# Eight weight matrices laid out slab by slab in HBM instead of row by row: a two-block kernel with 192 streamed 1 MB weight loads and 512 gathers

## The chip, the cores and the metric

The kernel runs on one core of a Trainium2 chip. The time is the device time of the whole program in microseconds (us), and less is better. One execution was also profiled, and the rows below are read from its trace.

## What is computed

One sequence of 256 tokens of width 2048, in fp32, goes through two blocks, one after the other.

```python
# first block
h = rms_norm(x, norm_gain);  proj = h @ w_in                      # 2048 x 8192
y_conv = rms_norm(short_gated_conv(...)) * silu(z_conv)           # 3 taps, width 1024
y_attn = rms_norm(moba_attention(q, k, v)) * silu(z_attn)         # 8 heads of 128
x = x + concat(y_conv, y_attn) @ w_out                            # 2048 x 2048
# second block
h = rmsnorm(x, norm_mix);  proj = h @ w_in_2                      # 2048 x 7168
merged = gate0 * (conformer_conv(...) @ conv_w_out)               # 1024 x 2048
       + gate1 * ((z @ ssm_w_val) * sigmoid(z @ ssm_w_gate))      # z from a grouped SSM
x = x + merged @ w_out_2                                          # 2048 x 2048
h = rmsnorm(x, norm_ffn)
q = h @ peer_w_q                                                  # 2048 x 2048
# per token 8 heads x top 16 experts of 16384: rows of u and v tables, 8 KB each
act = gelu(h . u_tab[expert]);  x = x + sum(gates * act * v_tab[expert])
return rmsnorm(x, norm_final)
```

## The kernel before

The 256 tokens are two tiles of 128. Everything but the last product keeps the channels on the partitions and the 256 tokens in the free dimension. The five engines run programs of their own that meet at semaphores; the order of all work is written out by hand.

**Weights.** The eight matrices `w_in`, `w_out`, `w_in_2`, `conv_w_out_2`, `ssm_w_val_2`, `ssm_w_gate_2`, `w_out_2` and `peer_w_q_2` are streamed through four buffers of 1 MB, `w_raw` (in the profile `weight_raw`, 128 partitions x 2048 floats), in 192 loads. A load is a slab: all rows of 128 columns of a matrix of 2048 rows, or of 256 columns of one of 1024 rows. `load` (L353) on SP's queue waits until TensorE has finished with the slab four before (`proj_done`), and issues one DMA. In HBM the matrices lie row by row, so that a partition gets 16 pieces of 512 bytes (8 of 1 KB for the matrices of 1024 rows). ACT (L766) makes a rounded copy `w_high` of most slabs, DVE (L1084) the rest `w_low`, in place, and TensorE multiplies three times (L495, L496, L499); 58 of the 216 tiles, those of `peer_w_q` among them, are plain fp32 products (L475).

**Start.** SP issues the two 1 MB loads of `x`, the first four slabs of `w_in` without a wait, then 16 loads of 32 KB and two of 256 KB for the SSM matrices, and the fifth slab once TensorE has finished the first. ACT's queue meanwhile issues 14 short loads of norm gains, biases and convolution taps (13 at L770 with 1 to 32 rows of 512 bytes, and at L789 the taps with 124 partitions of two rows), and three for the SSM. TensorE transposes `x` (L538), then waits for all 14 (`vec_in`, 16 * 14) and transposes them (L544); behind it in its program stand the 16 sums of squares of the first norm (L516), on which all else depends.

**The turn to the experts.** While TensorE makes the 16 tiles of `peer_w_q`, the keys of a head are scored as soon as its tiles are there (L716), ACT copies the scores (L766), and DVE picks the 16 best pairs (`head_picks`, from L1530). After heads 0, 3 and 7 the picks go out as row numbers (`experts`, L1570). POOL gathers one u row for each of 128 tokens with one indirect DMA of 1 MB (L435), and DVE makes its dot product (L1588). DVE's order is head 0, dots 0 to 2, head 1, dots 3 to 6, head 2, dots 7 to 9, head 3, dots 10 to 12, and so on. The gathers go to 7 row buffers at first and to 11 once the four weight buffers are free. As the slabs of `peer_w_q` are on the way meanwhile, POOL holds a gather back until a certain slab has landed:

```python
UNPACED = 3
def slab_before(s):
    return min(6 + (s - UNPACED) // 2, 15)
...
if UNPACED <= s < EARLY_PICKS:
    slab = SLAB_WQ + slab_before(s)
    pool.wait_ge(raw_landed[slab % NSLAB], 16 * (slab // NSLAB + 1))
```

Gathers 3 and 4 wait for slab 6 of `peer_w_q`, 5 and 6 for slab 7, 7 and 8 for slab 8, to 15. All in all there are 512 gathers: 128 of u and 128 of v for each tile of tokens. Half the v rows are summed by TensorE (L752) and half by DVE (L1606).

Of the kernel before, what the change touches and what calls it, by code (L numbers as in the profile page):

```python
# [13 lines left out]
P = 128  # L14
# [4 lines left out]
HALF = D // 2  # L19
KH = HALF // P  # L20
# [49 lines left out]
SLAB = 2048  # L70
NSLAB = 4
# [5 lines left out]
TILE_IN = 0  # L77
TILE_OUT = TILE_IN + 64
TILE_IN2 = TILE_OUT + 16
TILE_GATE = TILE_IN2 + 24  # L80
TILE_CV = TILE_IN2 + 56
TILE_VG = TILE_CV + 16
TILE_OUT2 = TILE_VG + 32
TILE_WQ = TILE_OUT2 + 16
# [41 lines left out]
def val(u):  # L126
# [3 lines left out]

BRANCH = [("glu", 0), ("sig", 0), ("glu", 1), ("sig", 1), *(("ssm", n) for n in range(4)),
          *((kind, n) for n in range(2, 8) for kind in ("glu", "sig")), *(("ssm", n) for n in range(4, 8))]
BRANCH_COL = {"glu": 0, "sig": HALF, "ssm": 2 * HALF}
BRANCH_SLOT = {"glu": GLU0, "sig": SIG0, "ssm": SSM0}
SUBK0, SUBT0 = 40, 16
TOPK0 = 48
# [43 lines left out]
def build(nc, d):  # L180
    ctx = ExitStack()
    with ctx:
        def sb(name, shape, dt=F32):
            return ctx.enter_context(nc.sbuf_tensor(name, shape, dt))

        def sem(name):
            return ctx.enter_context(nc.semaphore(name))
# [7 lines left out]
        w_raw = sb("weight_raw", [P, NSLAB, SLAB])  # L195
# [81 lines left out]
        raw_landed = [sem(f"raw_landed{b}") for b in range(NSLAB)]  # L277
# [59 lines left out]
        @block.sync  # L337
        def _(sp):
            for t in range(TT):
                sp.dma_start(x_tok0[:, t, :], d["x"][0, t * P:(t + 1) * P, :]).then_inc(x_in[t], 16)  # L340
            def matrix(name):
                return d[name][0].rearrange("(k p) n -> p k n", p=P)

            w_in, w_out, w_in2, w_val, w_gate, w_cv, w_out2, w_q = (matrix(n) for n in (
                "w_in", "w_out", "w_in_2", "ssm_w_val_2", "ssm_w_gate_2", "conv_w_out_2", "w_out_2", "peer_w_q_2"))

            def load(w, col, last_tile):

                at = len(slab_ends)
                if at >= NSLAB:  # L350
                    sp.wait_ge(proj_done, slab_ends[at - NSLAB])
                n = SLAB // w.shape[1]
                sp.dma_start(w_raw[:, at % NSLAB, :].rearrange("p (k n) -> p k n", n=n),  # L353
                             w[:, :, col:col + n]).then_inc(raw_landed[at % NSLAB], 16)
                slab_ends.append(last_tile)

            slab_ends = []
            for t in range(32):
                if t == NSLAB:
                    sp.wait_ge(cdiag_cleared, 1)  # L360
                    for c, name in enumerate(("ssm_c_re_2", "ssm_c_im_2")):
                        src = d[name][0].rearrange("(a g) h p -> g h a p", g=8)
                        for g in range(8):
                            sp.dma_start(c_diag[GCH * g:GCH * g + GCH, c, :, STATE * (g % 2):STATE * (g % 2) + STATE],
                                          src[g]).then_inc(c_in, 16)

                    sp.wait_ge(misc_done, M_X + 8)
                    for c, name in enumerate(("ssm_b_re_2", "ssm_b_im_2")):
                        sp.dma_start(b_nat[:, c, :, :], d[name][0].rearrange("(r s) p h -> (s p) r h", s=2)).then_inc(b_in, 16)
                load(w_in, 4 * HALF + P * t, TILE_IN + t + 1)  # L370
            for part in (0, 2, 1, 3):
                for t in range(KH):
                    load(w_in, part * HALF + P * t, TILE_IN + len(slab_ends) + 1)
            for t in range(16):
                load(w_out, P * t, TILE_OUT + t + 1)

            for t, (kind, n) in enumerate(BRANCH):
                load(w_in2, BRANCH_COL[kind] + P * n, TILE_IN2 + t + 1)
            for t in range(32):
                load(w_in2, 3 * HALF + P * t, TILE_GATE + t + 1)  # L380

            for j in range(8):
                load(w_cv, 256 * j, TILE_CV + 2 * j + 2)
            for u in range(8):
                for m, w in enumerate((w_val, w_gate)):
                    load(w, 256 * u, TILE_VG + 4 * u + 2 * m + 2)
            for t in range(4):
                load(w_out2, P * t, TILE_OUT2 + t + 1)

            sp.wait_ge(merged, KD)  # L390
            sp.dma_start(subk, d["peer_sub_keys_2"][0].rearrange("h c n e -> n (h c) e")).then_inc(subk_in, 16)
            for t in range(4, 16):
                load(w_out2, P * t, TILE_OUT2 + t + 1)
            for t in range(16):
                load(w_q, P * t, TILE_WQ + t + 1)

            sp.wait_ge(picks_ready, len(HEAD_PARTS) + 1)
            sp.dma_start(gain_b, d["norm_final_2"].partition_broadcast(P)).then_inc(gain_in, 16)
            for t in range(TT):
                for half in range(2):  # L400
                    cols = slice(half * HALF, (half + 1) * HALF)
                    sp.wait_ge(normed, 2 * t + half + 1)
                    sp.dma_start(d["out"][0, t * P:(t + 1) * P, cols], y_tok[:, t, cols]).then_inc(stored, 16)
            sp.wait_ge(stored, 16 * 2 * TT)
# [1271 lines left out]
]  # L1676


# [15 lines left out]
```

## Time and profile before

| | us |
|---|---|
| median of three runs | 2563.43 (2560.07 to 2563.51) |
| the profiled execution | 2563.8 |
| its span in the trace | 2562.0 |
| TensorE busy in the span | 1758.3 |
| VectorE (DVE) busy | 1840.4 |
| ScalarE (ACT) busy | 560.9 |
| GpSimd (POOL) busy | 871.9 |

The span runs from the first to the last instruction of the trace; 1.8 us of the execution lie around it. All times of rows are counted from the start of the span. A busy share over the whole span says little here, since the kernel has two halves of different kinds: up to about 1315 us the products, after that the gathers.

### The profile page before, as it was taken

What the parts mean: (1) busy time and instruction counts of PE and PEld (TensorE: products, weight loads), DVE (VectorE), ACT (ScalarE), POOL (GpSimd) and SP (SyncE); (2) the same over time, 40 slices, a digit from 0 to 9 for tenths busy, and PEclk for the clock granted to TensorE, in tenths of its full rate; (3) what the DMA queues carried; (4) which work ended last, traced back from release to release, by engine and by line L of the source; (5) the groups of instructions that cost most, each with busy time, mean ns of one, the idle gap of its engine ahead of it and who ended that gap; (6) DMA issues with size and microseconds to landing.
All of it is one profiled execution on the core that took longest, in us unless ns stands there. A gap on an engine that the chain in (4) does not pass through costs nothing. (4 is left out here: it accounts for less than half of the span.)

```text
span 2562.0 us, 25369 instructions
## 1 busy us (share of the span) xinstructions
PE 1758.3 (69%) x10238; PEld 1400.0 (55%) x10238; DVE 1840.4 (72%) x2417; ACT 560.9 (22%) x813; POOL 871.9 (34%) x525
## 2 busy tenths in 40 slices
PE   8999999999999979999950001776760000177776
PEld 7999999998899969999840000222220000022222
DVE  6655677476799896654799998778459999844444
ACT  4345555421036413433110000000000000000000
POOL 0000000000000000000348887565658888755552
PEclk9999999999999989999985555999995555599999
DMA  7655655655566535665999999999999999999997
GB/s 201 181 165 165 165 165 144 170 151 145 148 169 172 162 107 153 184 190 137 363 370 390 422 422 421 421 421 422 422 421 423 421 422 422 422 422 422 422 421 305
DMA packets 458296, 747.44 MB, mean 292 GB/s; under 512 B 22130, under 2 KB 391236, under 8 KB 392260
## 3 DMA queue, kind: packets, MB, share of 16 engines
q0 software_dynamic: 73728, 536.90, 50.5%
q1 hardware_dynamic: 383776, 208.68, 29.3%
q8 instruction: 81, 1.33, 0.2%
q10 hardware_dynamic: 676, 0.24, 0.0%
q14 instruction: 35, 0.29, 0.0%
HBM read 743.68 MB, written 2.10 MB: 291 GB/s over the span
## 5 line engine op out<-in xcount | busy, mean ns | idle before, releaser
L495 PE MATMUL ps<-operand_high,weight_high 128*128 128x256 f32 x2272 | 564.9, 288 | 6.7 <-DVE operand_low L1341 3.1
L496 PE MATMUL ps<-operand_low,weight_high 128*128 128x256 f32 x2272 | 555.3, 284 | 0.0
L1084 DVE TENSOR_TENSOR weight_low<-weight_raw,weight_high 128x2048 fp32r<-128x2048 f32 x142 | 325.3, 2291 | 199.2 <-ACT weight_high L766 198.7
L495 PEld LDWEIGHTS ps<-operand_high,weight_high 128*128 128x128 f32 x2272 | 438.3, 193 | 12.1 <-issue 7.0
L496 PEld LDWEIGHTS ps<-operand_low,weight_high 128*128 128x128 f32 x2272 | 438.6, 193 | 2.6 <-issue 2.2
L752 PE MATMUL ps<-weight_raw,residual_t 128*128 128x512 f32 x368 | 170.7, 607 | 327.2 <-ACT residual_t L1043 269.0
L427 POOL IOTA slots<- 128x16 f32 x1 | 0.1, 144 | 1071.9 <-DVE slots L1482 1071.9
L752 PE MATMUL ps<-rows_high,residual_t 128*128 128x512 f32 x192 | 91.4, 620 | 347.5 <-ACT residual_t L1043 316.0
L766 ACT ACTIVATE weight_high<-weight_raw 128x2048 fp32r<-128x2048 f32 x142 | 270.7, 1906 | 166.1 <-PE ps L499 101.7
L752 PEld LDWEIGHTS ps<-weight_raw,residual_t 128*128 128x128 f32 x368 | 67.0, 192 | 430.9 <-ACT residual_t L1043 339.1
L499 PE MATMUL ps<-operand_high,weight_low 128*128 128x256 f32 x2272 | 298.6, 283 | 1.7 <-DVE weight_low L1084 1.6
L499 PEld LDWEIGHTS ps<-operand_high,weight_low 128*128 128x128 f32 x2272 | 283.9, 192 | 2.2 <-DVE weight_low L1084 2.1
L752 PEld LDWEIGHTS ps<-rows_high,residual_t 128*128 128x128 f32 x192 | 35.8, 196 | 402.6 <-ACT residual_t L1043 344.1
L475 PE MATMUL ps<-slots,weight_raw 128*128 128x256 f32 x1088 | 240.1, 383 | 18.6 <-DVE slots L1457 17.1
L475 PEld LDWEIGHTS ps<-slots,weight_raw 128*128 128x128 f32 x1088 | 208.0, 192 | 49.7 <-issue 20.4
L1588 DVE SCALAR_TENSOR_TENSOR weight_raw<-weight_raw,work 128x2048 f32<-128x2048 f32 x85 | 193.3, 2290 | 13.8 <-DMA weight_raw<-in_peer_u,slots 13.5
L435 POOL DMA_INDIRECT weight_raw<-in_peer_u,slots x85 | 172.0, 2023 | 33.6 <-issue 24.4
L1588 DVE SCALAR_TENSOR_TENSOR slots<-slots,work 128x2048 f32<-128x2048 f32 x75 | 170.5, 2289 | 14.9 <-DMA slots<-in_peer_u,slots 14.7
L1606 DVE SCALAR_TENSOR_TENSOR work<-weight_raw,slots,work 128x2048 f32<-128x2048 f32 x45 | 105.8, 2352 | 91.9 <-DMA weight_raw<-in_peer_v,slots 91.6
L435 POOL DMA_INDIRECT slots<-in_peer_u,slots x75 | 145.7, 1943 | 61.9 <-DMA weight_raw<-in_peer_w_q 26.8
L819 ACT ACTIVATE slots<-ps 128x256 f32<-128x256 f32 x136 | 52.1, 383 | 500.7 <-PE ps L499 250.3
L435 POOL DMA_INDIRECT weight_raw<-in_peer_v,slots x91 | 129.1, 1419 | 93.6 <-PE ps L752 67.3
(220 smaller groups left out, 2510.5 us busy)
## 6 DMA issues: line engine op xcount, KB each, us to landing
weight_raw<-in_w_in SPq DMA_DIRECT2D x120, 1024.0 KB, 6.2
weight_raw<-in_w_out SPq DMA_DIRECT2D x32, 1024.0 KB, 5.9
weight_raw<-in_peer_w_q SPq DMA_DIRECT2D x16, 1024.0 KB, 12.0
weight_raw<-in_conv_w_out SPq DMA_DIRECT2D x8, 1024.0 KB, 5.6
weight_raw<-in_ssm_w_val SPq DMA_DIRECT2D x8, 1024.0 KB, 5.6
weight_raw<-in_ssm_w_gate SPq DMA_DIRECT2D x8, 1024.0 KB, 5.6
work<-in_x SPq DMA_DIRECT2D x2, 1024.0 KB, 6.2
out_y<-work SPq DMA_DIRECT2D x4, 512.0 KB, 5.2
```

What stands on the lines that cost most here:

```text
L427: nc.gpsimd.iota(iota16, pattern=[[1, 16]], base=0, channel_multiplier=0, allow_small_or_imprecise_dtypes=True).then_inc(zero_ready, 1)
L435: nc.gpsimd.indirect_dma_start(rows[b], None, table, bass.IndirectOffsetOnAxis(ap=picks[:, col:col + 1], axis=0),).then_inc(gathered[b], 16)
L475: mm = nc.tensor.matmul(ps_p[:, t % PSLOTS, :], w[:, k, :], operand[:, k, :], start=(k == order[0]), stop=(k == order[-1]))
L495: nc.tensor.matmul(out, high[:, k, :], o_high[:, place(k), :], start=(k == order[0]), stop=False)
L496: nc.tensor.matmul(out, high[:, k, :], o_low[:, place(k), :], start=False, stop=False)
L499: mm = nc.tensor.matmul(out, low[:, k, :], o_high[:, place(k), :], start=False, stop=(k == order[-1]))
L752: mm = nc.tensor.matmul(ps_v[:, c, :], diag[:, i // 2 % 16, :], rows[b][:, c * 512:(c + 1) * 512], start=False, stop=False, skip_group_che ...
L766: return nc.scalar.activation(dst, src, ACT.Copy)
L819: return nc.scalar.activation(dst, ps_p[:, n % PSLOTS, :], func, **kw).then_inc(proj_freed, 1)
L1084: v.tensor_tensor(w_low[:, s % NSLAB, :], w_raw[:, s % NSLAB, :], w_high[:, i % NHIGH, :], ALU.subtract).then_inc(w_low_ready, 1)
L1588: v.scalar_tensor_tensor(out=rows[b], in0=rows[b], scalar=1.0, in1=h_tok[:, t, :], op0=ALU.mult, op1=ALU.mult, accum_out=dots[:, at:at + 1 ...
L1606: v.scalar_tensor_tensor(out=y_tok[:, t, :], in0=rows[b], scalar=pick_w[:, at:at + 1], in1=y_tok[:, t, :], op0=ALU.mult, op1=ALU.add).then ...
```

## The change

The host lays each of the eight matrices out anew, once, ahead of the launch: slab after slab, and within a slab partition after partition with its 2048 floats (8 KB) in a row. The kernel's load takes slab number `slab` as it lies. The same bytes arrive at the same places of the same buffers; the order of the loads, their number and size, and all waits are the same, and no other load is changed.

```diff
-            def matrix(name):
-                return d[name][0].rearrange("(k p) n -> p k n", p=P)
-
-            w_in, w_out, w_in2, w_val, w_gate, w_cv, w_out2, w_q = (matrix(n) for n in (
+            w_in, w_out, w_in2, w_val, w_gate, w_cv, w_out2, w_q = (d[n] for n in (
                 "w_in", "w_out", "w_in_2", "ssm_w_val_2", "ssm_w_gate_2", "conv_w_out_2", "w_out_2", "peer_w_q_2"))
 
-            def load(w, col, last_tile):
+            def load(w, slab, last_tile):
 
                 at = len(slab_ends)
                 if at >= NSLAB:
                     sp.wait_ge(proj_done, slab_ends[at - NSLAB])
-                n = SLAB // w.shape[1]
-                sp.dma_start(w_raw[:, at % NSLAB, :].rearrange("p (k n) -> p k n", n=n),
-                             w[:, :, col:col + n]).then_inc(raw_landed[at % NSLAB], 16)
+                sp.dma_start(w_raw[:, at % NSLAB, :], w[slab]).then_inc(raw_landed[at % NSLAB], 16)
                 slab_ends.append(last_tile)
...
-                load(w_in, 4 * HALF + P * t, TILE_IN + t + 1)
+                load(w_in, 4 * KH + t, TILE_IN + t + 1)
...
+def in_slabs(w):
+
+    kts = w.shape[0] // P
+    n = SLAB // kts
+    return w.reshape(kts, P, w.shape[1] // n, n).transpose(2, 1, 0, 3).reshape(-1, P, SLAB)
...
-        a = np.ascontiguousarray(inputs[name])
+        a = np.ascontiguousarray(in_slabs(np.asarray(inputs[name])[0]) if name in _IN_SLABS else inputs[name])
```

The other calls of `load` go from columns to slab numbers in the same way.

## Rows read from the trace of the kernel before

**Rows 1.** The page's DMA queues: packets, MB, share of 16 engines' span

```profile
q0 software_dynamic: 73728, 536.90, 50.5%
q1 hardware_dynamic: 383776, 208.68, 29.3%
```

**Rows 2.** Windows: stretch, busy us (instructions) by engine, clock, DMA share, GB/s

```profile
200.00:300.00 100.00, 100.00 (x812) 98.20 (x811) 63.20 (x60) 56.33 (x79) 0.00 (x0) 1.00 0.61 167
...
2000.00:2200.00 200.00, 0.00 (x0) 0.00 (x0) 183.06 (x160) 0.00 (x0) 172.55 (x80) 0.50 1.01 422
```

**Rows 3.** Waits of TensorE up to 1300 us: total us, times, longest

```profile
PE ps L475 <- DVE slots L1457: 17.1, 1, 17.1
PE ps L538 <- DMA work<-in_x: 7.6, 2, 5.9
```

**Rows 4.** DMA issues of the whole span: count, KB each, median us to landing

```profile
weight_raw<-in_w_in SPq DMA_DIRECT2D x120, 1024.0 KB, 6.2
...
residual_t<-in_norm_final SPq DMA_DIRECT2D x1, 1024.0 KB, 9.1
```

**Rows 5.** Line 353 from 1160 to 1290: who waited for it (us, times), and landing

```profile
  POOL slots L435: 26.8, 3
...
  PEld ps L475: 0.3, 1
...
DMA to landing us min/median/max: 5.7/12.0/22.6
```

**Rows 6.** Line 353 from 1220 to 1228: slab 7 of `peer_w_q`

```profile
L353 SPq DMA_DIRECT2D weight_raw<-in_peer_w_q x1: 368/368/368, 1222.2 to 1222.2; - x1
...
DMA to landing us min/median/max: 16.8/16.8/16.8
```

**Rows 7.** Queues in the window 1230 to 1232 (q0 the gathers, q1 SP's)

```profile
q0 software_dynamic: 108, 0.77, 91.6%
q1 hardware_dynamic: 108, 0.06, 9.1%
```

**Rows 8.** POOL's timeline: gathers 5 and 35 (start, us, line, idle before)

```profile
1239.22 1.52 POOL L435 DMA_INDIRECT slots<-in_peer_u,slots  x1 [15.39 <-DMA weight_raw<-in_peer_w_q]
...
1344.90 2.74 POOL L435 DMA_INDIRECT operand<-in_peer_u,slots  x1 [11.26 <-DVE operand L1588]
```

**Rows 9.** DVE's timeline: dot 0, dot 5, and the first instruction of head 3

```profile
1223.65 2.29 DVE L1588 SCALAR_TENSOR_TENSOR rows_high<-rows_high,work 128x2048 f32<-128x2048 f32 x1 [6.17 <-DMA rows_high<-in_peer_u,slots]
...
1248.56 2.29 DVE L1588 SCALAR_TENSOR_TENSOR slots<-slots,work 128x2048 f32<-128x2048 f32 x1 [6.41 <-DMA slots<-in_peer_u,slots]
...
1265.83 0.29 DVE L1530 MAX8 slots<-residual_t 128x8 f32<-128x128 f32 x1
```

**Rows 10.** ACT's timeline: the copy of head 3's scores

```profile
1261.15 0.60 ACT L766 ACTIVATE residual_t<-ps 128x512 f32<-128x512 f32 x1 [0.51 <-PE ps L716]
```

**Rows 11.** ACT's queue in windows 2 to 6, 7.3 to 11, 11 to 13

```profile
q10 hardware_dynamic: 64, 0.02, 1.8%
...
q10 hardware_dynamic: 190, 0.06, 6.5%
...
q10 hardware_dynamic: 287, 0.12, 29.2%
```

**Rows 12.** SP's queue in the window 3 to 7.6, which holds `x` alone

```profile
q1 hardware_dynamic: 250, 1.90, 98.9%
```

**Rows 13.** PE's timeline at the start: parameter transposes, sums of squares

```profile
16.11 0.83 PE L544 MATMUL ps<-ident,slots 90*128 90x90 f32 x4 [0.87 <-DVE residual_t L1070]
16.78 7.08 PE L516 MATMUL ps<-scan_ws,ones 128*128 128x256 f32 x32
```

**Rows 14.** Line 789, the load of the taps: who waited for it

```profile
  PEld ps L544: 1.1, 1
```

**Rows 15.** Windows after an idle stretch of TensorE (columns as in rows 2)

```profile
938.00:940.00 2.00, 2.00 (x6) 1.58 (x5) 1.97 (x5) 0.00 (x0) 0.00 (x0) 0.50 0.00 0
...
944.00:946.00 2.00, 2.00 (x11) 1.77 (x10) 2.00 (x4) 0.00 (x0) 0.00 (x0) 1.00 0.00 0
```

More of the change, by code:

```diff
@@ L132 @@
           *((kind, n) for n in range(2, 8) for kind in ("glu", "sig")), *(("ssm", n) for n in range(4, 8))]
-BRANCH_COL = {"glu": 0, "sig": HALF, "ssm": 2 * HALF}
+BRANCH_SLAB = {"glu": 0, "sig": KH, "ssm": 2 * KH}
 BRANCH_SLOT = {"glu": GLU0, "sig": SIG0, "ssm": SSM0}
@@ L369, in _ @@
                         sp.dma_start(b_nat[:, c, :, :], d[name][0].rearrange("(r s) p h -> (s p) r h", s=2)).then_inc(b_in, 16)
-                load(w_in, 4 * HALF + P * t, TILE_IN + t + 1)
+                load(w_in, 4 * KH + t, TILE_IN + t + 1)
             for part in (0, 2, 1, 3):
                 for t in range(KH):
-                    load(w_in, part * HALF + P * t, TILE_IN + len(slab_ends) + 1)
+                    load(w_in, part * KH + t, TILE_IN + len(slab_ends) + 1)
             for t in range(16):
-                load(w_out, P * t, TILE_OUT + t + 1)
+                load(w_out, t, TILE_OUT + t + 1)
             for t, (kind, n) in enumerate(BRANCH):
-                load(w_in2, BRANCH_COL[kind] + P * n, TILE_IN2 + t + 1)
+                load(w_in2, BRANCH_SLAB[kind] + n, TILE_IN2 + t + 1)
             for t in range(32):
-                load(w_in2, 3 * HALF + P * t, TILE_GATE + t + 1)
+                load(w_in2, 3 * KH + t, TILE_GATE + t + 1)
             for j in range(8):
-                load(w_cv, 256 * j, TILE_CV + 2 * j + 2)
+                load(w_cv, j, TILE_CV + 2 * j + 2)
             for u in range(8):
                 for m, w in enumerate((w_val, w_gate)):
-                    load(w, 256 * u, TILE_VG + 4 * u + 2 * m + 2)
+                    load(w, u, TILE_VG + 4 * u + 2 * m + 2)
             for t in range(4):
-                load(w_out2, P * t, TILE_OUT2 + t + 1)
+                load(w_out2, t, TILE_OUT2 + t + 1)
             sp.wait_ge(merged, KD)
@@ L392, in _ @@
             for t in range(4, 16):
-                load(w_out2, P * t, TILE_OUT2 + t + 1)
+                load(w_out2, t, TILE_OUT2 + t + 1)
             for t in range(16):
-                load(w_q, P * t, TILE_WQ + t + 1)
+                load(w_q, t, TILE_WQ + t + 1)
             sp.wait_ge(picks_ready, len(HEAD_PARTS) + 1)
@@ L1676 @@
 ]
+_IN_SLABS = ("w_in", "w_out", "w_in_2", "conv_w_out_2", "ssm_w_val_2", "ssm_w_gate_2", "w_out_2", "peer_w_q_2")
+def in_slabs(w):
+    kts = w.shape[0] // P
+    n = SLAB // kts
+    return w.reshape(kts, P, w.shape[1] // n, n).transpose(2, 1, 0, 3).reshape(-1, P, SLAB)
 def kernel(**inputs):
```

## The prediction

> **What bounds the kernel now.** I began with the windows, because the slices of the page show two regimes. From 200 to 300 us TensorE is busy for all of the 100 us at a granted clock of 1.00, that is the 2.4 GHz level, while the DMA engines move 167 GB/s in 0.61 of the time. From 2000 to 2200 us TensorE is idle and the DMA engines are full at 422 GB/s [rows 2]. So there is a half that TensorE sets and a half that the gathers set. The queues give the pieces: SP's moves 208.68 MB in 383776 packets and takes 29.3% of 16 engines' span, the gathers 536.90 MB in 73728 packets and 50.5% [rows 1]. In 2562.0 us that is 208.68 / 751 = 278 GB/s while SP's queue is served, and 536.90 / 1294 = 415 GB/s for the gathers. Small pieces do cost engine time, some 750 us of it.
>
> The next question is who waits for those loads. TensorE's waits up to 1300 us hold 7.6 us for `x`, which the change doesn't touch, and 17.1 us for DVE, but no slab [rows 3]. A tile is 48 matmuls, and 812 of them in 100 us [rows 2] make 5.9 us a tile. A slab is issued when the tile four before it is done, and ACT, its first reader, comes to it when the tile two before it is done: 11.8 us later, while it lands in 6.2 [rows 4]. **Some 170 of the 192 loads are hidden, and making them faster is worth 0.** The cover is the four buffers; it is gone if a landing passes some 12 us.
>
> That leaves two places where a slab meets someone else's transfer: the turn to the experts, and the first 25 us.
>
> **Turn to the experts: a gain, -4.1 us.** Here 16 slabs share the engines with the gathers. Their landings take 12.0 us in the median and up to 22.6, and POOL waits for them, 26.8 us in three of its waits; TensorE only 0.3 [rows 5]. Slab 7 is issued at 1222.2 and takes 16.8 us, to 1239.0 [rows 6]. Gather 5 is held back for it and goes out at 1239.22 [rows 8], so DVE stands idle for 6.41 us before dot 5 at 1248.56 [rows 9]. Why 16.8? From 1230 to 1232 the two queues moved 108 packets each, but 0.77 MB against 0.06 [rows 7]: packet for packet, whatever their size. With 512-byte packets a slab gets a fourteenth of the bytes.
>
> With 8 KB packets it gets half. What a slab then takes I read from the only load of that shape beside gathers at full rate, `in_norm_final`: 9.1 us [rows 4]. Slab 7 lands at about 1231.3 and gather 5 goes out 8 us sooner. The price is that gathers 1 to 4 share their engines with it, 1 MB at 422 GB/s or 2.5 us for the last of them; for gathers 1 and 2, for which DVE waits too, I take 1.5 us. DVE is free for dot 5 at 1248.56 - 6.41 = 1242.15 today and would be at 1243.6. When dot 0's row has landed, at 1223.65 [rows 9], the engines have gathers 1 to 5 and two slabs to move, 7 x 1.05 MB at 422 GB/s or 17.4 us, so row 5 is there at 1241 to 1243. Dot 5 starts some 5 us sooner. This can't all be kept. Head 3 begins at 1265.83 now [rows 9], and its scores are copied by 1261.15 + 0.60 = 1261.75 [rows 10] at TensorE's pace, which doesn't change. **The cap is 1265.83 - 1261.75 = 4.1 us**, with about 1 us of slack against late rows. Behind head 3 DVE has no wait on a transfer, and gather 35, with which the full stretch opens, waits 11.26 us for DVE's dot [rows 8]. From there to the end the engines run at 422 GB/s, so the end moves by what DVE moves. Bounds: 0 (the rows come late by what POOL wins) and 4.1.
>
> **The first 25 us: a loss, +5.8 us.** Behind `x` SP's queue holds 4 slabs, 4.19 MB. Beside them run ACT's 14 short loads, and TensorE waits for all of them: the trace names the load of the taps as what its weight load of L544 waited for [rows 14], at 16.1 us [rows 13]. DVE's last copy is due at the same moment, so the taps may be up to 3 us early today: the bulk of them pass from 11 to 13 us (287 packets [rows 11]).
>
> How fast do short loads go? Between 2 and 6 us, beside the 8 KB packets of `x`, ACT's queue moved 64 packets, which are two loads of 16 rows (16 packets of data and 16 that signal, each): about 1.8 us a load. Between 7.3 and 11 us, beside 512-byte packets, it moved 190, which are the other ten: 0.37 us a load. The taps took 1.9 us from 11 to 13 [rows 11]. The change puts 8 KB packets in that second stretch. `x` moves 1.90 MB in 4.6 us, 0.413 MB per us [rows 12], so the four slabs are through at 7.6 + 4.19 / 0.413 = 17.8 us (today their last lands near 25.7, and nobody needs it sooner). Until then only (17.8 - 7.3) / 1.8 = 5.8 of the ten short loads have passed. The other 4.2 take 1.6 us at the quick pace, the taps 1.9, the landing about 0.5: 21.8 us. L544 starts 21.8 - 16.1 = 5.8 us later, rounded up, and as L516 and the whole chain of norm, scale and first product stand behind it in order, all of the first half moves by that. Bounds: 0 (the short loads keep their quick pace) and 8 (the small SSM loads, now queued right behind the slabs, hold them up too).
>
> The Trainium skill weighs on this place. Its page "DMA: Bandwidth & Descriptors", section on queues, rings and completion order, says that each engine goes round its queues packet by packet, a packet holding some 9 to 17 descriptors. Rows 7 agree with the round, not with the size, as single pieces alternate there. By that rule a turn would hold a slab's eight rows on one engine, hardly a short load would get past before the slabs are through, and the start would slip to 17.8 + 10 x 0.37 + 1.9 + 0.5 = 23.9 us: 7.8 instead of 5.8, and a sum of +6.1 instead of +4.1, inside the bounds below and above.
>
> **The clock, +2.4 us.** That delay leaves TensorE idle from about 15.2 to 21.8 us. After its idle 17.1 us of rows 3, which end at about 937, it did 6 matmuls in 2 us at a granted clock of 0.50 (1.2 GHz), and 11 in 2 us at 1.00 from 944 on [rows 15]. So the low level loses 5/11 of the time that it lasts under work, here 4 to 6 us, which is 1.8 to 2.7. L516 keeps TensorE busy for 7.08 us [rows 13] and would take that on itself. I take 2.4. Bounds 0 (the clock doesn't fall) and 3.
>
> **Sum.** 0 - 4.1 + 5.8 + 2.4 = +4.1 us. On the profiled execution's 2563.8 (span 2562.0 and 1.8 around it) this is 2567.9. That execution was 0.4 above the median of the runs, so I predict 2567.5.
>
> **The rivals.**
> 1. *The short loads land in time.* If ACT's queue is not held up, nothing moves at the start, and the clock term falls with it: 2563.4 - 4.1 = 2559.3. For it: up to 3 us of slack, and the speed of the taps once they come, 287 packets in 2 us [rows 11]. Against: 1.8 us a load beside `x`. The point that decides is the landing of the last of the 14 at 16.1 us. Chance 0.18. This one ends on the other side of no change.
> 2. *The gathers lose what they win.* Half the engines' time goes to each slab while it is in flight, so rows 1 to 6 come late, and DVE waits there instead of at dot 5. Then only the loss stands: 2563.4 + 8.2 = 2571.6. It decides if dot 5 can't start before 1248. Chance 0.12.
> 3. *Layout gives no speed.* If 512 bytes are as good as 8 KB, all is as before: 2563.4. Against it stand 278 and 415 GB/s [rows 1]. The engines might owe that to something else than piece size, so chance 0.07. The Trainium skill has a rule for this rival: the same page's specifications give 512 bytes as the least transfer for the line rate. Rows 1 disagree.
> 4. *TensorE sees the bursts.* A slab now arrives in under 3 us of engine time rather than about 4. If this slowed readers of the same partitions, 1150 us of products would stretch; 0.5% is 6 us, so 2573. No row speaks for it. Chance 0.05.
>
> **How the numbers follow.** My forecast has 0.55, with its own range of 2564 to 2570 from the bounds of start and clock; 0.03 is left for what I don't see. Rivals 1 and 3 lie inside 0.2% of the median (2558.3 to 2568.6; about what a measurement of this kernel can tell from no change), and of my own case some two thirds do (0.38 of 0.55). Rivals 2 and 4 are slower. Faster than 2558.3 is only a corner of rival 1, if head 3's scores come earlier too, 0.05, and most of what I don't see, 0.02. That gives faster 0.07, same 0.60 (0.38, 0.13 of rival 1, 0.07 and a rest), slower 0.33. The range takes in rival 1 at the lower end and rival 2 at the upper: 2559 to 2572.
>
> **What would show it.** In the profile after: SP's queue has about 39700 packets (192 slabs go from 368640 pieces to 24576) in place of 383776, for the same bytes; a slab beside nothing lands in 4 to 5 us. L544 starts near 21.8, and L516 takes over 9 us instead of 7.08; the granted clock is 0.50 in the windows around 22 us. If L544 still starts at 16.1, rival 1 holds. Around the turn, everything counted from the start of the first `peer_w_q` tile: slab 7 lands after about 9 us, DVE's wait before dot 5 is under 1 us, and head 3 waits for its scores instead. TensorE's gaps between 100 and 900 us stay the same to 1 us. If POOL is still held back by 10 us or more, the packet rule that I take from rows 7 is wrong for pieces of equal size.

## The result, and the profile after

The changed kernel took 2567.81 us (median of 13 runs, 2566.18 to 2569.82), the kernel before 2563.43 beside it (13 runs, 2559.57 to 2564.72). The ratio is 1.0021 with a 95% interval of 1.0012 to 1.0029: slower by 4.4 us, where +4.1 was forecast. Its profiled execution took 2567.72 us, with a span of 2565.9. That the sum came out does not show that its terms did. The profile shows each of them.

The page's DMA queues of the changed kernel, and below them the issues with their landings (columns as in rows 1 and 4):

```profile
q0 software_dynamic: 73728, 536.90, 50.5%
q1 hardware_dynamic: 39712, 208.68, 24.1%
...
weight_raw<-in_w_in SPq DMA_DIRECT2D x120, 1024.0 KB, 4.9
...
weight_raw<-in_peer_w_q SPq DMA_DIRECT2D x16, 1024.0 KB, 8.7
```

The packets are the 39700 that were expected. The same bytes take 24.1% of the span instead of 29.3% [rows 1], and a slab lands in 4.9 us instead of 6.2 [rows 4]. The transfers did get faster: 0.052 x 2562 = 133 us of engine time were saved. Hardly any of it is time of the kernel, because TensorE hardly ever waited for a slab (0.3 us at the turn [rows 5]).

**The start.** TensorE's timeline of the changed kernel from 0 to 40 us: `x` is transposed (L533), then the parameters (L539, formerly L544), then come the sums of squares (L511, formerly L516) and the first product (L470, formerly L475).

```profile
8.59 6.36 PE L533 MATMUL ps<-ident,work 128*128 128x128 f32 x28 [1.79 <-DMA work<-in_x]
22.43 1.31 PE L539 MATMUL ps<-ident,slots 90*128 90x90 f32 x4 [7.49 <-DMA slots<-in_conv_w_dw]
23.54 9.04 PE L511 MATMUL ps<-scan_ws,ones 128*128 128x256 f32 x32
...
35.68 4.56 PE L470 MATMUL ps<-slots,weight_raw 128*128 128x256 f32 x20 [0.42 <-DVE slots L1090]
```

The parameter transposes begin at 22.43 and not at 16.11 [rows 13]. TensorE has stood idle for 7.49 us, and the row names what it waited for, the load of the taps. Then even the transposes take 1.31 us for 0.83, and the sums 9.04 for 7.08. The windows say why (stretch, busy us and instructions by engine, then the granted clock, the DMA share and GB/s):

```profile
16.00:18.00 2.00, 0.00 (x0) 0.00 (x0) 0.00 (x0) 0.00 (x0) 0.11 (x1) 0.82 1.00 401
...
24.00:26.00 2.00, 2.00 (x6) 1.64 (x5) 0.56 (x4) 0.83 (x2) 0.00 (x0) 0.50 0.44 31
26.00:28.00 2.00, 2.00 (x7) 1.59 (x7) 0.00 (x0) 0.90 (x3) 0.00 (x0) 0.62 0.73 75
28.00:30.00 2.00, 2.00 (x11) 1.77 (x10) 0.00 (x0) 1.94 (x5) 0.00 (x0) 1.00 0.68 63
```

From 16 to 18 us no engine but the DMA works, apart from 0.11 us of POOL, and the DMA is full. The granted clock is 0.50 (1.2 GHz) in the windows in which TensorE comes back and the next, and is back at 1.00 (2.4 GHz) from 28 us on. Together the first product starts 8.7 us late, at 35.68 instead of 26.96. Of this, 22.43 - 16.11 = 6.3 are the wait and 2.4 the clock.

**The turn.** DVE's timeline of the changed kernel: head 0's first instruction, dots 2 and 5, head 3's first instruction.

```profile
1216.15 0.49 DVE L1525 MAX8 slots<-residual_t 128x8 f32<-128x128 f32 x2 [13.03 <-ACT residual_t L761]
...
1240.08 2.29 DVE L1583 SCALAR_TENSOR_TENSOR operand<-operand,work 128x2048 f32<-128x2048 f32 x1 [2.62 <-DMA operand<-in_peer_u,slots]
...
1252.43 2.29 DVE L1583 SCALAR_TENSOR_TENSOR slots<-slots,work 128x2048 f32<-128x2048 f32 x1
...
1269.98 0.48 DVE L1525 MAX8 slots<-residual_t 128x8 f32<-128x128 f32 x2
```

Head 0 is 8.02 us late (1208.13 before). Dot 5 has no idle time in front of it, where it had 6.41 us [rows 9], and head 3 begins at 1269.98 instead of 1265.83, only 4.15 us late. So the turn gives back 8.02 - 4.15 = 3.87 us. POOL's timeline tells where it is from, and how the end follows:

```profile
1240.48 2.69 POOL L430 DMA_INDIRECT slots<-in_peer_u,slots  x1 [8.65 <-DMA weight_raw<-in_peer_w_q]
...
1349.08 2.75 POOL L430 DMA_INDIRECT operand<-in_peer_u,slots  x1 [11.27 <-DVE operand L1583]
```

Gather 5 is held back for 8.65 us, not 15.39, and gather 35, with which the full stretch opens, goes out 4.18 us later than before [rows 8]. From there on the engines move 422 GB/s in both kernels, and the end comes 2565.9 - 2562.0 = 3.9 us later.

### The profile page after: what moved, and what is told of

It is laid out like the page before. It is cut to its first block and busy times, and to the rows that moved or that the text cites. A ratio compares the mean times of both kernels' runs of the same rounds, so it can differ in the third digit from the quotient of the medians.

```text
span 2565.9 us, 25369 instructions
## 1 busy us (share of the span) xinstructions
PE 1765.3 (69%) x10238; PEld 1403.8 (55%) x10238; DVE 1840.4 (72%) x2417; ACT 561.2 (22%) x813; POOL 877.5 (34%) x525
## 3 DMA queue, kind: packets, MB, share of 16 engines
q1 hardware_dynamic: 39712, 208.68, 24.1%
## 5 line engine op out<-in xcount | busy, mean ns | idle before, releaser
L470 PE MATMUL ps<-slots,weight_raw 128*128 128x256 f32 x1088 | 239.3, 382 | 18.5 <-DVE slots L1452 17.0
L470 PEld LDWEIGHTS ps<-slots,weight_raw 128*128 128x128 f32 x1088 | 207.5, 191 | 49.4 <-issue 20.4
```

Source lines behind the costliest of these rows:

```text
L470: mm = nc.tensor.matmul(ps_p[:, t % PSLOTS, :], w[:, k, :], operand[:, k, :], start=(k == order[0]), stop=(k == order[-1]))
```

## The experiments

Each kernel below was timed in turns with the kernel before on one chip. The theory on record is that two effects of opposite sign add up: a loss at the start, because short loads wait behind the first four slabs, and a gain at the turn, because slabs get half the bytes beside gathers. The rivals say that one of the two is something else, or that the 172 loads in between cost something.

The table shows where the effects sit in each profiled execution (starts from the timelines, us). The last columns are how far the median is from that of the kernel before in the same batch (2562.35, 2562.63 and 2562.02 us in the three), and the ratio with its interval.

| kernel | first product | head 0 to head 3 | median, difference | ratio |
|---|---|---|---|---|
| before | 26.96 | 57.70 | | |
| after | 35.68 | 53.83 | 2567.81, +4.4 | 1.0021 [1.0012, 1.0029] |
| first four slabs old | 26.77 | 53.67 | 2557.98, -4.4 | 0.9987 [0.9978, 0.9996] |
| slabs held back | 26.68 | 53.65 | 2558.58, -3.8 | 0.9986 [0.9977, 0.9995] |
| `peer_w_q` old | 35.14 | 57.44 | 2571.33, +9.0 | 1.0039 [1.0025, 1.0052] |
| both old | 27.04 | 57.59 | 2562.71, +0.4 | 1.0001 [0.9992, 1.001] |
| two slabs held back | 26.12 | 53.69 | 2558.25, -4.4 | 0.9985 [0.9976, 0.9994] |
| held back, no pacing | 26.38 | 53.89 | 2558.61, -4.0 | 0.9985 [0.9976, 0.9994] |
| 60 fillers | 38.70 | 54.38 | 2571.06, +8.4 | 1.0033 [1.002, 1.0045] |
| 33 fillers | 33.90 | 53.65 | 2565.42, +3.4 | 1.0014 [1.0005, 1.0023] |
| pieces of 2 KB | 31.97 | 55.66 | 2565.32, +3.3 | 1.0016 [1.0007, 1.0025] |
| blocks, pieces of 512 | 26.74 | 57.27 | 2563.02, +0.4 | 1.0003 [0.9994, 1.0012] |
| before, held back | 26.96 | 57.48 | 2562.17, +0.2 | 0.9998 [0.9989, 1.0007] |

**1. The slabs held back.** The changed kernel, whose SP waits for the 14 short loads before its first slab. This takes away the collision and leaves every layout as it is.

```diff
+                if t == 0:
+                    sp.wait_ge(vec_in, 16 * 14)
                 load(w_in, 4 * KH + t, TILE_IN + t + 1)
```

> The changed kernel, but SP waits until all 14 short loads of ACT's queue have landed before it issues the first slab. Theory (the short loads crawl beside 8 KB packets of the slabs; gain of about 3.9 us at the turn to the experts stays): the parameter transposes start at DVE's pace, 16 us, the sums of squares take 7.1 us again, and the time is 2567.8 - 8.7 = 2559 us, below the kernel before by some 4. Rival (the loss comes from something else in the start, the SSM loads or the slabs' bursts): stays near 2567.

TensorE's timeline of this kernel, and ACT's and SP's queue from 7.3 to 11 us (packets, MB, share):

```profile
15.83 0.83 PE L541 MATMUL ps<-ident,slots 90*128 90x90 f32 x4 [0.88 <-DVE residual_t L1067]
16.50 7.08 PE L513 MATMUL ps<-scan_ws,ones 128*128 128x256 f32 x32
```

```profile
q1 hardware_dynamic: 28, 0.10, 6.5%
q10 hardware_dynamic: 553, 0.21, 27.3%
```

With SP's queue quiet, ACT's moves 553 packets in these 3.7 us, where it moved 190 beside slabs of 512-byte pieces [rows 11] and 140 beside those of 8 KB. The slabs go out from 10.69 us on and are still in time. The wait for the taps and the low clock are both gone, and the turn keeps its 4 us. The loss at the start is the collision, and it costs nothing to avoid.

**2. Only the first four slabs old.** They come row by row from a second copy of `w_in`.

```diff
-                load(w_in, 4 * KH + t, TILE_IN + t + 1)
+                load(w_in if t >= 4 else d["w_in_rows"], 4 * KH + t, TILE_IN + t + 1)
```

> The changed kernel, but the first four slabs come from a copy of w_in that lies row by row, in pieces of 512 bytes; the other 188 in rows of 8 KB. Theory: no loss at the start, the whole gain at the turn: 2559 to 2560 us, as when the slabs are held back. Rival: the loss is spread over the product half (bursts of 8 KB disturb readers), then 2567.

The same time by another way, with the SSM loads where they were: 4 of 192 loads carry the whole loss.

**3. `peer_w_q` old, all else new.** Its 16 loads take 512-byte pieces again.

```diff
-                load(w_q, t, TILE_WQ + t + 1)
+                load(w_q[0], t, TILE_WQ + t + 1)
```

> The changed kernel, but peer_w_q lies row by row as before. Theory: the loss at the start stays, the gain at the turn goes: 2567.8 + 3.9 = 2571.7 us, and DVE waits some 6.4 us before dot 5. Rival (the turn gained nothing, the start cost less): 2567.8.

DVE's timeline of this kernel at dot 5:

```profile
1256.38 2.29 DVE L1587 SCALAR_TENSOR_TENSOR slots<-slots,work 128x2048 f32<-128x2048 f32 x1 [6.23 <-DMA slots<-in_peer_u,slots]
```

The wait of 6.41 us [rows 9] is back, as 6.23, and the loss stands alone, +9.0. So the gain of the turn is in the layout of `peer_w_q`.

**4. Both old.** The edits of 2 and 3 together; the 172 loads in between keep their 8 KB rows.

> The changed kernel, but the first four slabs and peer_w_q lie row by row; 172 loads in between in rows of 8 KB. Theory (these loads are hidden, piece size is worth 0 there): as the kernel before, 2563.4 us within 1. Rival (bursts of 8 KB slow the products): above 2564.5.

The ratio is 1.0001. The 172 faster loads are worth nothing that can be measured, and neither do their denser bursts cost anything: the interval is -2.0 to +2.6 us.

**5. Fillers against the clock.** The changed kernel, in which TensorE does unused matmuls before it waits for the short loads.

```diff
+            keep_clock(60)
             pe.wait_ge(vec_in, 16 * 14)
```

> The changed kernel with 60 small matmuls of the constants on TensorE (7 us, results unused) ahead of its wait for the 14 short loads, so that it isn't idle meanwhile. Theory (the low clock after the idle stretch costs 2.0 us of the 8.7, as the sums of squares take 9.04 us in place of 7.08 and the parameter transposes 1.3 in place of 0.8): sums of squares at 7.1 us, 2567.8 - 2.4 = 2565.4 us. Rival (the clock term isn't on the path): 2567.8.

A miss: 2571.06 us where 2565.4 was expected. TensorE's timeline of this kernel:

```profile
14.48 13.56 PE L500 MATMUL ps<-ident,ones 128*128 128x128 f32 x120
27.88 0.81 PE L540 MATMUL ps<-ident,slots 90*128 90x90 f32 x4
28.53 7.08 PE L511 MATMUL ps<-scan_ws,ones 128*128 128x256 f32 x32
```

The 60 fillers were meant to fill the idle time, but took 13.56 us, twice what I had reckoned, and delayed the transposes by 27.88 - 22.43 = 5.4 us themselves. Still the sums take 7.08 us: the clock had not fallen. So the first product is only 38.70 - 35.68 = 3.0 us later than in the changed kernel, and the time is +8.4 for its +4.4. To see the clock alone, the next kernel has 33:

> The changed kernel with 33 of the small matmul pairs ahead of TensorE's wait for the short loads: 7.5 us of work, as 60 of them took 13.56. Theory: the transposes start at 22.4 as in the changed kernel, and the clock holds, so 0.5 + 1.96 us come back: 2567.8 - 2.4 = 2565.4 us. Rival (a side effect of the fillers cost the 3.3 us of the run with 60, not their length): 2567.8 or more.

```profile
14.66 7.53 PE L500 MATMUL ps<-ident,ones 128*128 128x128 f32 x66
23.03 0.86 PE L540 MATMUL ps<-ident,slots 90*128 90x90 f32 x4 [0.83 <-DMA slots<-in_conv_w_dw]
23.73 7.08 PE L511 MATMUL ps<-scan_ws,ones 128*128 128x256 f32 x32
```

The same timeline with 33. The transposes still wait for the taps, and start 0.6 us later than in the changed kernel. But they take 0.86 us for 1.31, the sums 7.08 for 9.04, together 2.4 less, and the first product comes 35.68 - 33.90 = 1.8 us sooner, which is 2.4 less the 0.6. That is the clock's term, read from the timeline. The medians of the two kernels are 2.4 apart, but they were not timed in one batch, and against the kernel before it is +3.4 for +4.4; the intervals of the ratios overlap. The time agrees with the sign and can't fix the size.

**6. Two slabs held back.** Slabs 0 and 1 go out at once, 2 and 3 after the short loads (`if t == 2` in the edit of 1). By the terms of my prediction the short loads would still be late.

> SP issues slabs 0 and 1 at once and slabs 2 and 3 once the 14 short loads have landed. Theory by its own terms: two slabs are through at 12.7 us, 2.8 of ten short loads have passed, the others take 2.7 us, the taps 1.9, the landing 0.5: parameter transposes at 17.8 us, no clock loss, 2559 + 1.7 = 2560.7 us; 2559.0 if the short loads go quicker with nothing beside them. Rival (it is the mere presence of 8 KB packets, not how many): as the changed kernel, near 2567.

L541 starts at 15.27 and not at 17.8, with DVE's last copy as what it waits for, and the time is 2.4 us below what my terms gave. The short loads were no longer late at all, so my pace of 1.8 us a load beside 8 KB packets is wrong. What is right in its place is told below.

**7. Held back, and no pacing.** The edit of 1, and POOL doesn't hold gathers back for slabs any more:

```diff
-                            if UNPACED <= s < EARLY_PICKS:
-                                slab = SLAB_WQ + slab_before(s)
-                                pool.wait_ge(raw_landed[slab % NSLAB], 16 * (slab // NSLAB + 1))
```

> The held slabs, and POOL no longer waits for slabs of peer_w_q before gathers 3 to 27. Theory (a slab in 8 KB rows gets half the engines beside gathers, so TensorE never waits, and DVE is capped by the scores of head 3, which it misses by 0.2 us): 2558.6 us within 0.5. Rival (the pacing is still needed: the gathers hold the slabs up and TensorE waits): slower by several us.

The time is that of 1 within the interval. The pacing was there to protect slabs of small pieces from the gathers; that it was needed there is not shown, since no run took it out of the old layout. With 8 KB rows it is not needed: the slabs of `peer_w_q` land in 8.6 us in the median without it, and TensorE waits for none.

**8. Where the gain in speed is: pieces of 2 KB.** Each slab as four parts, so that a partition reads 4 pieces of 2 KB.

```diff
-                sp.dma_start(w_raw[:, at % NSLAB, :], w[slab]).then_inc(raw_landed[at % NSLAB], 16)
+                sp.dma_start(w_raw[:, at % NSLAB, :].rearrange("p (c f) -> p c f", c=4),
+                             w[:, slab].rearrange("c p f -> p c f")).then_inc(raw_landed[at % NSLAB], 16)
```

> Each slab in four pieces of 2 KB per partition, the four a large stride apart in HBM. Theory if each piece is a packet: beside 2 KB packets ACT's queue passes four times as many of its own as beside 8 KB ones, so the parameter transposes start at 16 to 17 us, and a slab of peer_w_q gets a fifth of the bytes beside gathers, lands about 3 us sooner than with 512 bytes: 2560 to 2561.5 us, below the kernel before. Rival (four pieces are sent as one packet): as the changed kernel, 2567.8. Rival (only whole rows of 8 KB gain anything): 2563.4.

A miss: 2565.32 us where 2560 to 2561.5 was expected. Its queue and landing on the page and in the issues, TensorE's timeline, and DVE's at dot 5:

```profile
q1 hardware_dynamic: 113440, 208.68, 23.9%
...
weight_raw<-in_w_in SPq DMA_DIRECT2D x120, 1024.0 KB, 5.1
```

```profile
19.07 1.31 PE L540 MATMUL ps<-ident,slots 90*128 90x90 f32 x4 [4.11 <-DMA slots<-in_conv_w_dw]
20.18 8.70 PE L512 MATMUL ps<-scan_ws,ones 128*128 128x256 f32 x32
```

```profile
1250.08 2.29 DVE L1584 SCALAR_TENSOR_TENSOR slots<-slots,work 128x2048 f32<-128x2048 f32 x1 [3.33 <-DMA slots<-in_peer_u,slots]
```

The engine time is all there (23.9% against 24.1%), but I had expected the short loads in time, and they are 3 us late, with the clock term behind them. The first product is 5.0 us late, the turn gives 57.70 - 55.66 = 2.0 back, which makes +3.0; +3.3 was measured. Both effects grow with the piece, the loss not slower than the gain.

**9. Blocks, but pieces of 512.** A slab is one block of 1 MB in HBM, and inside it the rows lie as before. This parts "one block" from "long pieces".

```diff
-                sp.dma_start(w_raw[:, at % NSLAB, :], w[slab]).then_inc(raw_landed[at % NSLAB], 16)
+                sp.dma_start(w_raw[:, at % NSLAB, :].rearrange("p (k n) -> p k n", k=w.shape[1]),
+                             w[slab].rearrange("k p n -> p k n")).then_inc(raw_landed[at % NSLAB], 16)
```

> Each slab is one block of 1 MB in HBM as in the changed kernel, but within it the rows of 128 (256) columns stand one after another, so that a partition again gets pieces of 512 bytes (1 KB). Theory (the size of the packets decides, not where the slab lies): as the kernel before, 2563.4 us within 1, parameter transposes at 16.1 us, DVE idle some 6.4 us before dot 5. Rival (the place in HBM decides): as the changed kernel, 2567.8.

Its queue on the page, the landing, and the two queues from 1230 to 1232:

```profile
q1 hardware_dynamic: 125728, 208.68, 29.2%
...
weight_raw<-in_w_in SPq DMA_DIRECT2D x120, 0.5 KB, 6.3
```

```profile
q0 software_dynamic: 83, 0.56, 74.4%
q1 hardware_dynamic: 86, 0.18, 23.8%
```

No gain in engine time (29.2% as against 29.3% [rows 1]): to lie in one block brings nothing, the piece decides. But the packets are a third in number, some 2 KB each, and they go in turns with the gathers' packets, 86 to 83. So the piece sets what a byte costs an engine, and, beside gathers, the packet sets what share a queue gets. With 0.18 MB in 2 us instead of 0.06 [rows 7] slab 7 ought to have come sooner, but it comes hardly sooner: POOL issues gather 5 21.0 us after gather 0 (21.5 in the kernel before, 14.7 in the changed one), and DVE waits 5.36 us before dot 5. The start was not delayed.

**10. The kernel before, held back.** The wait of 1 in the kernel before, as a control.

> The kernel before, old layout, with SP waiting for the 14 short loads before its first slab, a control for the same edit in the new layout. Theory (beside 512-byte packets the short loads were in time anyway): 2563.4 us within 0.7. Rival (holding the slabs back is itself a gain of some us, whatever the layout): 2560.

0.9998: the wait by itself brings nothing beyond the interval. The gain of run 1 is the layout's.

## Why the prediction was right, and where its terms were not

*Hidden loads, 0.* Right. Both old gives 1.0001 with 172 loads in the new layout, and in the changed kernel the way from the first product to head 0 takes 1180.5 us for 1181.2.

*The turn, -4.1.* Right in place and size: 3.87 between head 0 and head 3, and 3.8 to 4.05 in the four kernels whose start is undisturbed. Putting back `peer_w_q` alone takes it away (57.44 against 57.70). But it isn't the cap that made the size. I had taken 1.5 us as the price of late rows, which leaves 5 of the 6.41 us, more than the cap of 4.1 lets through. The price was 2.3: counted from head 0, dot 2 starts at 23.9 us for 21.6 before. What is left of the wait is then 4.1, and 0.3 more idle time before dot 6 makes it 3.8. That this agrees with the cap is luck. The cap itself lay 0.2 us further: ACT's copy of head 3's scores is done at 1269.17 + 0.60 = 1269.77, and DVE comes at 1269.98, so head 3 did not wait for its scores, though I had written that it would. The slab landed in 10.0 us where I had 9.1. The two queues move equal bytes at the turn, from 1234 to 1236 us of the changed kernel:

```profile
q0 software_dynamic: 59, 0.43, 53.1%
q1 hardware_dynamic: 47, 0.39, 47.0%
```

*The first 25 us, +5.8.* Right in place (the four kernels that disarm it are at -3.8 to -4.4) and nearly in sum, with 6.3, but not in its working. The queues of the changed kernel from 11 to 13 us, from 15 to 17, from 17 to 19, and from 19 to 21:

```profile
q1 hardware_dynamic: 107, 0.77, 93.5%
q10 hardware_dynamic: 74, 0.02, 5.0%
...
q1 hardware_dynamic: 116, 0.82, 101.5%
q10 hardware_dynamic: 58, 0.01, 3.6%
...
q1 hardware_dynamic: 685, 0.55, 101.7%
q10 hardware_dynamic: 28, 0.01, 3.4%
...
q1 hardware_dynamic: 1099, 0.25, 123.3%
q10 hardware_dynamic: 143, 0.07, 20.6%
```

I had 5.8 of the ten short loads through when the slabs end, and then a quick rest. In fact 448 of ACT's 676 packets were past by 17 us (the windows added up), and all ten are among them: the 13 loads ahead of the taps have 154 pieces, and the 154th piece of 512 bytes in ACT's queue passes at 12.0 us, for 10.6 in the kernel before. It was the taps that crept. **The step that failed is the price of 1.8 us a load, read beside `x`, and the 1.9 us that I took for the taps.**

The sizes and times of ACT's single packets in the trace show why. The last load of ACT's queue, the third one for the SSM, has 32 pieces of 8 bytes. Of these 24 pass by 15.5 us, and the other 8 only from 21.4 us on, behind the taps. So on twelve of the 16 engines nothing of the taps stood in the way, and four engines carry them: 248 pieces, 62 on each. On such an engine the pieces pass in turns with SP's. The queues of the changed kernel from 16 to 18 us, then of run 8 from 14 to 17 and of run 9 from 11 to 13:

```profile
q1 hardware_dynamic: 114, 0.79, 97.4%
q10 hardware_dynamic: 24, 0.01, 2.2%
...
q1 hardware_dynamic: 503, 1.00, 99.3%
q10 hardware_dynamic: 101, 0.05, 6.6%
...
q1 hardware_dynamic: 212, 0.40, 82.8%
q10 hardware_dynamic: 277, 0.11, 28.5%
```

In the first, 96 of SP's 114 packets are rows of 8 KB, 6 on each of 16 engines, and ACT's 24 are taps, 6 on each of four: one piece for one row, and a row takes an engine 0.32 us. In run 8 it is 25 pieces for 30 of 2 KB, in the kernel before, from 11 to 13 us, 58 for 50 of 512 bytes. So the taps need 62 turns, and a turn is as long as SP's packet. At 18 us some 175 of the 248 are still to come. When the slabs are through, at 18.4 us, ACT's queue moves 71 pieces per us instead of 12. Run 6 fits: its two slabs are through at 12.7 us, when the taps begin. This is worked out from traces; no run spread the taps over more engines. From 17 to 19 the last slab and the small pieces of the SSM loads share SP's queue, so part of the loss may be theirs, as my upper bound of 8 had it. Two errors offset each other, a price too high for the small loads and too low for the taps, and the sum is nearer than its parts deserve.

The Trainium skill's page "DMA: Bandwidth & Descriptors", in its section on queues, rings and completion order, has some 9 to 17 descriptors to a packet, by which the prediction put the slip at 7.8; 6.3 was measured. The turns of one piece for one row don't agree with it; run 9's packets do hold several pieces, but four each.

*The clock, +2.4.* Right: 2.4 at the first product, and with 33 fillers transposes and sums take 2.4 us less.

*The rivals.* Short loads in time: refuted by the wait of 7.49 us; it is what the kernel with held slabs does, at -3.8 for the -4.1 worked out. Gathers lose what they win: they lose 2.3 us, and the turn still gives 3.87; run 3, without the gain, has that rival's time, +9.0 for +8.2. No speed from layout: refuted by 24.1%. TensorE sees the bursts: run 4 leaves 2.6 us for it at most, where 6 were named.

**Open.** The loss at the first product is 8.7 us, at head 0 8.0; between these two points the profiles scatter by 1178.8 to 1181.2 us without order, and I can't say why. Why four pieces go into one packet in run 9 but not in the kernel before isn't settled. Nor is what such a packet counts for: beside gathers it is one turn (86 to 83), but at the start, from 11 to 13 us, some 4 of ACT's pieces pass for one of them (217 on four engines, 54 on each, against 196 on 16, 12 on each). That is how run 9's start stays in time while run 8's, with single pieces of 2 KB, doesn't.

## What to carry to other kernels

Before a transfer is made faster, ask which queue it shares engines with: the weights got 18% cheaper in engine time here, which was worth 3.9 us at 16 of 192 loads and nothing at the rest, and TensorE got the 14 short loads beside the first four of them 6.3 us late, which with the clock cost 8.7. Ask also how many engines a short load is spread over: the one that came last passed on four of 16, a piece at a turn. A bulk load that nobody needs yet can be held back behind the short ones that somebody does; that one wait turned 1.0021 into 0.9986, and the changed kernel with it beats both. And a pacing that was written for small pieces should be tried again without, once they are large.

## What the runs showed of the hardware

- In pieces of 2 KB the weights cost no more engine time than in rows of 8 KB (23.9% and 24.1% of the span for 208.68 MB); in pieces of 512 bytes it is 29.2 or 29.3%. A slab of `w_in` lands in 5.1, 4.9 and 6.2 us in the median.
- A short load's 512-byte pieces on four engines passed at 12 per us beside another queue's rows of 8 KB (24 in 2 us), at 34 beside pieces of 2 KB (101 in 3 us), and ACT's at 117 beside pieces of 512 bytes (234 in 2 us), although that queue carried 0.24 MB in all.
- Pieces and packets are two things: in one layout of the same 512-byte pieces SP's queue had 383776 packets [rows 1], in another 125728, at the same cost in engine time.
- 60 fillers, 120 matmuls of fp32 128x128 in the trace, took 13.56 us, 0.11 us each. While TensorE did them its clock stayed up, and the sums behind them took 7.08 us instead of 9.04.
